# Transposes moved from TensorE and PSUM to DMA: a two-layer retention and sliding-window step on eight cores

## What is computed

```python
def retention_chunk(S, q, k, v, lg):          # chunks of 128 tokens, 4 heads, key 256, value 512
    scores = einsum('bihd,bjhd->bhij', q, k) * decay          # decay[i,j] = exp((i-j)*lg), i >= j
    o = einsum('bhij,bjhe->bihe', scores, v)
    o = o + einsum('bihd,bhde->bihe', q * exp((idx+1)*lg), S)
    k_dec = k * exp((C-1-idx)*lg)
    S_new = exp(C*lg) * S + einsum('bjhd,bjhe->bhde', k_dec, v)
# retention_mixer: y = (silu(g) * rms_norm(o)) @ w_out
# attention: q, k = rope(rms_norm(q, q_gain)), rope(rms_norm(k, k_gain)); 16 query and 4 key heads of 64
#   y = softmax([q k^T / 8, sink]) v @ w_out, window 128
# every block: x = x + mixer(rms_norm(x, gain)); x = x + swiglu(rms_norm(x, gain))
```

## Time and profile before

| | us |
|---|---|
| median of 3 runs (2007.52 to 2010.4) | 2008.47 |
| the profiled execution's own time | 2006.02 |
| its span, slowest core (core 7) | 2004.5 |
| spans of the 8 cores | 1994.1 to 2004.5 |
| PE busy, share of the span | 1886.5, 94% |
| DVE, ACT, POOL busy | 1083.5, 740.9, 258.7 |
| mean granted TensorE clock, core 7 | 0.979 |

### The profile page before, as it was taken

The page is one execution under the profiler, slowest core; times in us unless marked ns, Lnnn a source line. Parts: engine busy times, 40 slices in busy tenths (PEclk is TensorE's granted clock), DMA queues, the critical chain, the costliest instruction groups (busy, mean ns, idle before and its releaser), DMA issues.

```text
span 2004.5 us, 30003 instructions; the slowest of 8 cores (1994.1 to 2004.5 us)
## 1 busy us (share of the span) xinstructions
PE 1886.5 (94%) x10850; PEld 876.3 (44%) x10850; DVE 1083.5 (54%) x1544; ACT 740.9 (37%) x1201; POOL 258.7 (13%) x463
## 2 busy tenths in 40 slices
PE   4889999989989989999999998989989999999998
PEld 1434444434434434444444444444444444444444
DVE  3668677767758754334334467665653333343444
ACT  3555454455446761111111155665665111111111
POOL 2211101101111120000000014332331000000000
PEclk9889999999989999999999999999999999999999
DMA  9745743653552450533024113000064031240113
GB/s 183 186 106 133 159 122 112 161 130 125 137 137 103 121 143 15 96 50 64 12 37 60 20 33 64 1 1 4 1 90 64 1 64 22 42 64 0 33 43 132
DMA packets 103823, 153.80 MB, mean 77 GB/s; under 512 B 6464, under 2 KB 56640, under 8 KB 103616
## 3 DMA queue, kind: packets, MB, share of 16 engines
q0 software_dynamic: 59920, 59.91, 20.3%
q1 hardware_dynamic: 43760, 91.97, 13.9%
HBM read 167.08 MB, written 48.76 MB: 108 GB/s over the span
## 4 chain that ended last, share of the span: by engine, by line
PE 84%; DVE 4%; issue 4%; ACT 4%; DMA 2%; POOL 1%; SPq 0%; DVEq 0%; ACTq 0%; POOLq 0%
PE PS L705 81%; ACT R L719 4%; PE PS L711 3%; DVE R L726 3%; DVE R L736 1%; POOL R L726 1%; DMA R<-w_ret_out 1%; DMA R<-w_ffn_in 1%; DMA ss_out<-R 1%; DMA R<-xp 0%; DMA R<-state 0%; POOL R L730 0%; SPq L203 0%; POOL R L203 0%; DVE R L740 0%
## 5 line engine op out<-in xcount | busy, mean ns | idle before, releaser
L705 PE MATMUL PS<-R 128*128 128x512 bf16 (+7 forms) x9568 | 1826.8, 353 | 61.0 <-ACT R L719 32.5
L705 PEld LDWEIGHTS PS<-R 128*128 128x128 bf16 (+3 forms) x9568 | 796.9, 99 | 997.2 <-issue 204.6
L726 DVE TENSOR_TENSOR R<-R,PS 128x1024 f32<-128x1024 f32 (+3 forms) x530 | 484.5, 921 | 616.8 <-PE PS L705 586.1
L719 ACT ACTIVATE R<-PS 128x512 bf16<-128x512 f32 (+7 forms) x674 | 413.0, 626 | 1088.8 <-PE PS L705 999.2
L719 ACT ACTIVATE R<-R 128x1024 bf16<-128x1024 f32 (+3 forms) x302 | 289.3, 972 | 137.1 <-DVE R L726 57.7
L726 DVE TENSOR_TENSOR R<-PS,R 128x1024 bf16<-128x1024 bf16 (+7 forms) x270 | 179.2, 682 | 171.9 <-PE PS L705 105.2
L711 PE MATMUL PS<-R 128*128 128x128 bf16 (+1 forms) x1282 | 127.0, 225 | 50.6 <-ACT R L719 31.3
L736 DVE SCALAR_TENSOR_TENSOR R<-PS,R 128x512 f32<-128x512 f32 (+2 forms) x224 | 137.8, 638 | 59.7 <-POOL R L726 35.7
L726 POOL TENSOR_TENSOR R<-R 128x1 f32<-128x1 f32 (+5 forms) x238 | 150.3, 638 | 108.9 <-DVE R L726 86.4
L736 DVE SCALAR_TENSOR_TENSOR R<-R,PS 128x1024 f32<-128x1024 f32 x124 | 147.7, 1217 | 27.6 <-PE PS L705 17.3
L711 PEld LDWEIGHTS PS<-R 128*128 128x128 bf16 (+1 forms) x1282 | 87.8, 101 | 124.3 <-issue 98.3
(11 more groups left out here) (19 smaller groups left out, 42.2 us busy)
## 6 DMA issues: line engine op xcount, KB each, us to landing
R<-state SPq DMA_DIRECT2D x64, 512.0 KB, 4.3
ss_out<-R SPq DMA_DIRECT2D x64, 512.0 KB, 3.0
R<-w_ffn_in POOLq DMA_DIRECT2D x16, 1024.0 KB, 11.5
R<-xp SPq DMA_DIRECT2D x16, 512.0 KB, 13.8
R<-w_ret_in POOLq DMA_DIRECT2D x8, 1024.0 KB, 12.1
R<-w_ffn_out POOLq DMA_DIRECT2D x8, 1024.0 KB, 9.6
yp<-R SPq DMA_DIRECT2D x16, 512.0 KB, 3.8
R<-w_ffn_in POOLq DMA_DIRECT2D x8, 768.0 KB, 8.9
```

The costliest lines, as they stand in the source:

```text
L705: o = self.P.op("pe", lambda e: e.matmul(real(out), lhsT=lhsT, rhs=rhs, start=start, stop=stop), reads, writes, dur=max(0.029, self._fsz(o ...
L719: return self.P.op("act", lambda e: e.activation(out=real(out), in_=real(in_), func=func, **kw), reads, writes, dur=(0.38 if "accum_out" i ...
L726: return self.P.op(eng, lambda e: e.tensor_tensor(out=out, in0=real(in0), in1=real(in1), op=op), reads, writes, dur=self._vd(out, eng))
```

## The change

A new helper `dtr` issues a transposing DMA from SBUF to SBUF on SP's queue, with one of 8 semaphores ("xt") in turn. It replaces the PE transposes and the copy out of PSUM in five places: norms 1, 2 and 3 (DMA from hb into HT, then the gain product in place in HT, by DVE in norm 2 and by POOL in norms 1 and 3), gated heads, retention keys, attention's queries and keys, and attention's outputs. Norm 0, the sample keys of retention and the cached keys of attention keep PE. Since a DMA cannot scale, the decay of a key moves into the ACT copy of v; the mask decT, which v now meets too, becomes a constant per head on and above the diagonal. Keys are laid out chunk by chunk (kr), gated and oTg get two buffers each, the gate buffer sg4 two instead of four, and `gn_tr` is called right after `gn_elem` instead of a chunk later. The planner has a pipe of its own for these DMAs, at twice the rate.

```diff
-                s0 = max(st + 1.6, pipe[0])
-                pipe[0] = s0 + o.nbytes / DMA_RATE
-                fin = pipe[0] + 0.5
+                pi_ = 1 if o.slot[0] == "xt" else 0
+                s0 = max(st + 1.6, pipe[pi_])
+                pipe[pi_] = s0 + o.nbytes / DMA_RATE / (1 + pi_)
+                fin = pipe[pi_] + 0.5
...
-        decT[:, h, :] = np.where(diff >= 0, np.exp(-(i[:, None] + 1.0) * lg[h]), 0.0)
+        decT[:, h, :] = np.where(diff >= 0, np.exp(np.float32(-128.0) * lg[h]), 0.0)
...
+    def dtr(self, out, in_, reads, writes):
+        self.ndtr = (self.ndtr + 1) % 8
+        return self.P.dma("sp", out, in_, slot=("xt", self.ndtr), reads=reads, writes=writes, transpose=True)
...
+            if gi > 0:
+                ht = self.HT[:, :, t * 128:t * 128 + n]
+                self.dtr(ht, hb[0:n, :], [hk], [("HT", t)])
+                self.tt(ht, ht, self.gainT[:, gi, :].unsqueeze(2).broadcast_to([128, 8, n]), ALU.mult, [("HT", t), "gainT"], [("HT", t)],
+                        eng="dve" if gi == 2 else "pool")
+                return
...
-        kr = [A(f"kr{i}", [2, 512], BF16) for i in range(2)]
+        kr = [A(f"kr{i}", [4, 2, 128], BF16) for i in range(2)]
         ta = A("ta", [512], F32); tb = A("tb", [512], F32)
-        vc = [A(f"vc{i}", [512], BF16) for i in range(2)]; sg4 = A("sg4", [4, 512], BF16)
+        vc = [A(f"vc{i}", [512], BF16) for i in range(2)]; sg4 = A("sg4", [2, 512], BF16)
...
-        gated = A("gated", [512], BF16); oTg = A("oTg", [4, 128], BF16)
+        gateds = [A(f"gated{i}", [512], BF16) for i in range(2)]; oTgs = [A(f"oTg{i}", [4, 128], BF16) for i in range(2)]
...
+            gated, gk_ = gateds[i], f"gated{i}"
+            gq_.append(i)
             r_ = rst[:, i, :]; rk = ("rst", i)
-            self.act(gated[0:n, :], src, AF.Square, o_keys, ["gated", rk], scale=RDV ** -0.5, accum_out=r_[0:n, 0:1])
...
-                     o_keys + [rk, sgkey], ["gated"])
...
+                     o_keys + [rk, sgkey], [gk_])
...
         def gn_tr(n):
-            ti, tk = self.bank()
-            pb = self.psb(ti).rearrange("p (a b) -> p a b", a=8)
-            for ec in range(4):
-                self.tr(pb[:, ec, 0:n], gated[0:n, ec * 128:(ec + 1) * 128], ident[0:n, 0:n], ["gated", "ident"], tk)
-            self.act(oTg[:, :, 0:n], pb[:, 0:4, 0:n], AF.Copy, tk, ["oTg"])
+            i = gq_.pop(0)
+            oq_.append(i)
+            self.dtr(oTgs[i][:, :, 0:n], gateds[i][0:n, :], [f"gated{i}"], [f"oTg{i}"])
...
+            oi_ = oq_.pop(0)
+            oTg, otk = oTgs[oi_], f"oTg{oi_}"
...
-            rope(bi, bk, 512, tok0, kr[s % 2], f"kr{s % 2}", 1.0 / 16.0)
+            rope(bi, bk, 512, tok0, kr[s % 2].rearrange("p c a q -> p a c q"), f"kr{s % 2}", 1.0 / 16.0)
...
             bi, bk = proj_tm(f"rg{h}", 128, cidx * 128, [("HT", cidx)])
-            self.act(sg4[:, cidx % 4, :], self.psf(bi), AF.Silu, bk, [("sg4", cidx % 4)])
...
-                ti, tk = self.bank()
-                pb = self.psb(ti).rearrange("p (a b) -> p a b", a=8)
-                for hf in range(2):
-                    self.tr(pb[:, hf, :], kb[:, hf, c0:c0 + 128], ident, [kbk, "ident"], tk)
-                self.act(ktb, pb[:, 0:2, :].rearrange("p a b -> p (a b)"), AF.Copy, tk + ["kcol"], [ktk], scale=kcol[:, h:h + 1])
+                self.dtr(ktb.rearrange("p (a b) -> p a b", a=2), kb[:, cc, :, :].rearrange("p a b -> p (a b)"), [kbk], [ktk])
                 bi, bk = proj_tm(f"rv{h}", 128, cidx * 128, [("HT", cidx)])
-                self.act(vcb, self.psf(bi), AF.Copy, bk, [vck])
+                self.act(vcb, self.psf(bi), AF.Copy, bk + ["kcol"], [vck], scale=kcol[:, h:h + 1])
...
-                    self.mm(self.psf(si)[:, 0:128], kb[:, hf, c0:c0 + 128], qb[:, hf, c0:c0 + 128], hf == 0, hf == 1, [kbk, qbk], sk_)
+                    self.mm(self.psf(si)[:, 0:128], kb[:, cc, hf, :], qb[:, hf, c0:c0 + 128], hf == 0, hf == 1, [kbk, qbk], sk_)
...
-                if prev is not None:
-                    gn_tr(128)
...
                 gn_elem(128, oi, ok_, sgb, sgk, h)
+                gn_tr(128)
...
         def front_tr(n, fr, kT, kTk, qT, qTk):
             q_r, qrk, kd, kdk = fr
-            ti, tk = self.bank()
-            pb = self.psb(ti).rearrange("p (a b) -> p a b", a=8)
-            for m in range(2):
-                self.tr(pb[:, m, 0:n], kd[0:n, 2 * m:2 * m + 2, :].rearrange("p a b -> p (a b)"), ident[0:n, 0:n], [kdk, "ident"], tk)
-            self.act(kT, pb[:, 0:2, 0:n], AF.Copy, tk, [kTk])
-            ti, tk = self.bank()
-            pb = self.psb(ti).rearrange("p (a b) -> p a b", a=8)
-            for cc in range(8):
-                self.tr(pb[:, cc, 0:n], q_r[0:n, cc, :, :].rearrange("p a b -> p (a b)"), ident[0:n, 0:n], [(qrk, cc // 4), "ident"], tk)
-            self.act(qT, pb[:, :, 0:n], AF.Copy, tk, [qTk])
+            self.dtr(kT[:, :, 0:n], kd[0:n].rearrange("p a b -> p (a b)"), [kdk], [kTk])
+            self.dtr(qT[:, :, 0:n], q_r[0:n].rearrange("p a b c -> p (a b c)"), [(qrk, 0), (qrk, 1)], [qTk])
...
         def o_tr(n_):
             oT, oTk = oTs[0], "oT0"
             o_n, onk = o_ns[0], "o_n0"
-            ti, tk = self.bank()
-            pb = self.psb(ti).rearrange("p (a b) -> p a b", a=8)
-            for cc in range(8):
-                self.tr(pb[:, cc, :], o_n[:, cc, :, :].rearrange("p a b -> p (a b)"), ident, [(onk, cc // 4), "ident"], tk)
-            self.act(oT, pb, AF.Copy, tk, [oTk])
+            self.dtr(oT, o_n.rearrange("p a b c -> p (a b c)"), [(onk, 0), (onk, 1)], [oTk])
```

More of the change, by code:

```diff
@@ L287, in schedule @@
         last_form = [0]
-        pipe = [0.0]
+        pipe = [0.0, 0.0]
         total = len(allops)
@@ L634, in __init__ @@
         self.uid = 0
+        self.ndtr = 0
     def inp(self, name, shape):
@@ L958, in retention @@
         gcnt = [0]
+        gq_ = []
+        oq_ = []
         pend_nb = []
@@ L964, in rope @@
             a = ta[:, 0:n]; b_ = tb[:, 0:n]
+            o0, o1 = out[:, 0], out[:, 1]
+            av, bv = (a, b_) if len(out.shape) == 3 else (a.rearrange('p (c q) -> p c q', c=4), b_.rearrange('p (c q) -> p c q', c=4))
             self.stt(a, x1, scale, cs, ALU.mult, ALU.mult, [keys[0], ("rcos", tok0 // 512)], ["ta"])
             self.stt(b_, x2, scale, sn, ALU.mult, ALU.mult, [keys[1], ("rsin", tok0 // 512)], ["tb"])
-            self.tt(out[:, 0, 0:n], a, b_, ALU.subtract, ["ta", "tb"], [outkey])
+            self.tt(o0, av, bv, ALU.subtract, ["ta", "tb"], [outkey])
             self.stt(a, x2, scale, cs, ALU.mult, ALU.mult, [keys[1], ("rcos", tok0 // 512)], ["ta"])
             self.stt(b_, x1, scale, sn, ALU.mult, ALU.mult, [keys[0], ("rsin", tok0 // 512)], ["tb"])
-            self.tt(out[:, 1, 0:n], a, b_, ALU.add, ["ta", "tb"], [outkey])
+            self.tt(o1, av, bv, ALU.add, ["ta", "tb"], [outkey])
         def proj_fm(wname, n, tok0, htkeys):
@@ L992, in gn_elem @@
             gcnt[0] += 1
+            gated, gk_ = gateds[i], f"gated{i}"
+            gq_.append(i)
             r_ = rst[:, i, :]; rk = ("rst", i)
-            self.act(gated[0:n, :], src, AF.Square, o_keys, ["gated", rk], scale=RDV ** -0.5, accum_out=r_[0:n, 0:1])
+            self.act(gated[0:n, :], src, AF.Square, o_keys, [gk_, rk], scale=RDV ** -0.5, accum_out=r_[0:n, 0:1])
             self.rsq(r_[0:n, 2:3], r_[0:n, 0:1], n, [rk], epsc[0:n, ecol:ecol + 1], ["epsc"])
             self.stt(gated[0:n, :], src, r_[0:n, 2:3], sgbuf[0:n, :], ALU.mult, ALU.mult,
-                     o_keys + [rk, sgkey], ["gated"])
+                     o_keys + [rk, sgkey], [gk_])
         def gn_tr(n):
-            ti, tk = self.bank()
-            pb = self.psb(ti).rearrange("p (a b) -> p a b", a=8)
-            for ec in range(4):
-                self.tr(pb[:, ec, 0:n], gated[0:n, ec * 128:(ec + 1) * 128], ident[0:n, 0:n], ["gated", "ident"], tk)
-            self.act(oTg[:, :, 0:n], pb[:, 0:4, 0:n], AF.Copy, tk, ["oTg"])
+            i = gq_.pop(0)
+            oq_.append(i)
+            self.dtr(oTgs[i][:, :, 0:n], gateds[i][0:n, :], [f"gated{i}"], [f"oTg{i}"])
         def gn_out(h, n, xt):
             wo = self.W[f"ro{h}"]
+            oi_ = oq_.pop(0)
+            oTg, otk = oTgs[oi_], f"oTg{oi_}"
             if n == NS:
-                self.pair_out(xt, lambda i: wo[:, i, :], lambda i: ["oTg", self.wkey[f"ro{h}"]], lambda i: oTg[:, i, 0:n], 4)
+                self.pair_out(xt, lambda i: wo[:, i, :], lambda i: [otk, self.wkey[f"ro{h}"]], lambda i: oTg[:, i, 0:n], 4)
             else:
@@ L1194, in retention @@
         self.free("rcos", "rsin", "decT", "epsc", "kcol", "sdec", "rowmask", "qr0", "qr1", "kr0", "kr1", "ta", "tb",
-                  "vc0", "vc1", "sg4", "sTm0", "sTm1", "ktok0", "ktok1", "gated", "oTg", "Sf", "Sb", "rst", "qr_s", "kr_s",
+                  "vc0", "vc1", "sg4", "sTm0", "sTm1", "ktok0", "ktok1", "gated0", "gated1", "oTg0", "oTg1", "Sf", "Sb", "rst", "qr_s", "kr_s",
```

6 lines of the change are left out of this document (3 added, 3 removed).

## The result

The changed kernel takes **2075.59 us** (median of 4 runs, lowest 2073.72) against 2007.99 us for the kernel before on the same chip (4 runs): ratio **1.033**, 95% interval 1.031 to 1.035. The forecast was 1973 us. The profiled execution has a span of 2074.9 us on core 3, against 2004.5 before: +70.4. In the cores' list the mean granted clock of TensorE is 0.952 to 0.957, before 0.977 to 0.982. Some runs of a kernel are far slower, with a lower mean clock on one half of the chip or on both; ratios leave those out, and a time called "compared" is the median of the runs that its ratio uses.

What follows compares the result with a forecast made beforehand. The prediction took PE to bind almost everywhere; -57 - 10 + 5 + 6 + 20 = -36 us against 2006.0 gave 1970, and with 2.5 for the median of the runs 1973 us, range 1937 to 2110.

Steps and rivals of the forecast that it cites:

- PE's share, -57 us: On PE's path: 1106 of 1282 transposing instructions go, at 52 ns each, 57 us gained.
- The gain on ACT's waits (-10): PE's waits before transposes and attention matmuls, partly for copies of transposed tiles: 10 us gained, ends 0 and 24.
- Landing 3.5 and 3.0 us: Transposing DMAs on SP's queue: assumed landing of a 128x1024 tile and of a gated head's 128x512 tile.
- the packet rival (8.1 us): Transposes pay by the packet: 128x1024 lands in 8.1 us, 128x512 in 4.9; kernel 2112 us; chance 0.26.
- how much does PE tolerate: Room for a transpose's landing, from PE's order: 3.1 us at attention outputs, 2.3 and 3.4 us at gated heads.
- These 26 us of stall: PE's forecast stalls for transposes: 20 us at gated heads, 6 us at attention outputs, 0 at norms and keys.
- POOL's gain product, 5 us: 34 products of 128x1024 on POOL, some 2.5 us each, costing 5 us in all; ends 0 and 30.
- SP's issue, 0.38 us each: SP's time to issue each of 233 transposes, taken from plain DMAs; nobody waits for it at that price.
- SP blocks in retention: Rival: transposes behind state loads in SP's order cost 56 us instead of 6, about 2023 us; chance 0.14.
- either end that I drew from the Trainium skill: Two pages on 128x1024 transposes: 10.5 us and about 2160 us in all, or 1.0 us and about 1945.
- my own list: Expected signs: 176 L711 left, landings 2.5 to 4 us, small DMA waits, faster attention, unchanged feed-forward.
- The signs that were to show the forecast wrong: Median landing above 4.2 us, SP's queue busy most of an attention block, or retention waits over 60 us.

Runs made afterwards that it cites:

- e8: Changed kernel with only the gated heads' transposes back on TensorE: 2044.6 us compared, ratio 1.015 to the kernel before.
- e3: Changed kernel, same order, weight pieces from the ninth on loading only their first row block: 2019.44 us, ratio 1.006.
- e4: Kernel before the change, own order, weight pieces from the ninth on loading only their first row block: 1999.7 us compared, ratio 0.997.
- e5: Changed kernel, planner counting transposing DMAs in the one pipe of all DMAs, without the halved time per byte: 2015.03 us, ratio 1.000.
- e6: Changed kernel with the gain products of norms 1 to 3 left out: 2052.62 us, ratio 1.018.
- e13: Changed kernel with its separate planner pipe kept, only SP's planned time per transpose set to 1.2 us: 2085.95 us, ratio 1.030.
- e9: Changed kernel with one shared planner pipe and SP's planned time per transpose set to 1.2 us: 2007.01 us, ratio 0.990.
- e15: The kernel of e9 again with more rounds: 1998.17 us (6 runs), ratio 0.989 to the kernel before.

## Why the prediction was wrong

- **PE's share, -57 us:** right. 176 instructions are left, and the busy time gives 47. The gain on ACT's waits (-10) came in part and was lost elsewhere: ACT's row before ordinary matmuls falls from 16.8 us to 11.7 in attention, but grows from 32.5 to 41.6 over the span.
- **Landing 3.5 and 3.0 us:** right as a median (3.1 over all), and so the packet rival (8.1 us) fell, though it had the sign. The pieces are 256-byte packets as it feared, 1024 for a 128x1024 tile. But if the whole growth of q1's share is theirs, it gives (0.245 × 2074.9 - 0.139 × 2004.5) × 16 / 145,824 = 0.025 us for one, a quarter of the 0.102 it took from the long packets.
- **The step that failed** is "how much does PE tolerate": "Stall of gated heads: 19 × (3.0 + 0.35 - 2.3) = 20 us, the second group 0", and 6 for attention outputs, 0 for norms and keys "unless the queue itself is full". These 26 us of stall were the term that failed. PE stood 58.9 to 69.3 us for transposes directly, gated heads came to 31 + 14 = 45 us by e8, and PE's idle time grew by 106.6 in all. Two things are in it. I set one usual landing against each distance, and where weight pieces were in flight the landings shown took 11 to 16 us; with the weights thinned 47 of the 67 us were gone (e3, e4). And even then PE stood 38.5 to 46.1 us for transposes, so the distances of this order didn't cover shorter landings either; how these waits split over gated heads, keys, norms and outputs isn't shown. The trace of the kernel before had two warnings. A state load's median of 4.3 us hid a longest of 9.6 to 13.1 over the cores (80 to 800 us), and these pieces were on POOL's queue, which I didn't take as the company of a transpose:

```profile
R<-w_ffn_in POOLq DMA_DIRECT2D x16, 1024.0 KB, 11.5
R<-w_ret_in POOLq DMA_DIRECT2D x8, 1024.0 KB, 12.1
```

- **The order wasn't questioned.** The distances were read from the changed kernel's order, but that order was made by a planner that in the same diff had been told that transposes never queue behind other transfers. Put right, the same instructions take 60 us less (e5). It was in the diff and had no term or rival.
- **POOL's gain product, 5 us:** its duration was right (2.0 against 2.5), the wait in front was not: 23 us (e6), within my ends of 0 and 30, and 6 once the order is mended.
- **SP's issue, 0.38 us each:** measured 1.2, and up to 9.0 under weight pieces. Mending it in the plan alone takes back none of the 67 us (e13), but 8 to 17 once the pipe is right (e9, e15); what the issue time itself costs on the chip wasn't isolated. The rival "SP blocks in retention" had the right engine and the wrong wait: SP's wait for stored states fell from 163.4 us to 31.6.
- **The clock** had no term. More idle time goes with a lower mean grant (0.952 to 0.957 against 0.977 to 0.982); the same matmuls took 10.5 us more beside it. In e15 the same matmuls take 1816.7 us at a mean of 0.965 (its core 6), less than before at 0.979, so mean clock and matmul time don't go together one to one, and no more is claimed.
- **The pages.** The trace doesn't bear out either end that I drew from the Trainium skill. "VectorE: DVE Perf Modes", section "The three transpose paths", gives 1309 ns for 128x128; eight squares landed in 3.1 us, not in proportion. "DMA: Bandwidth & Descriptors", section "Latency and other measured facts", gives 261 GB/s for transposes with a non-contiguous middle dimension; 64 packets of 0.025 us on each of 16 engines are an estimate of 1.6 us for 256 KB, or 160 GB/s, beside this kernel's other transfers.

By my own list, 1106 fewer, the landing and the full feed-forward parts came true; PE's waits for DMA in attention (16.6 us against "under 15") and in retention (51.3 against "under 30") did not, and attention took 9.5 us more instead of less. The signs that were to show the forecast wrong, a median landing above 4.2 us or over 60 us of waits in retention, didn't come either: a median can't show a tail, and less than 60 us was enough to lose.

**Open:** why the issue of a transpose holds SP for up to 9 us while weight pieces fly. The long landing isn't peculiar to transposes. Over the eight cores the longest landing of a state load in retention was 9.6 to 13.1 us in the kernel before, 10.1 to 11.6 in the changed one, and 6.0 to 7.9 in it with thin weights (each from 80 us on), all at medians near 4. But the issue of a state load took 1.9 us at most in the changed kernel. Fewer small packets per transpose or weight pieces in smaller parts weren't tried.

## What to carry to other kernels

Price a transfer that stands on the path by its landing in the company that it keeps, not by the median: look up which large loads are in flight where its reader waits, and the longest landing of a plain load there. When a change moves work to another engine and also edits the planner's costs, test the two apart first; here the moved work was worth some 10 us of gain under a sound plan, and the planner's edit cost 60. And a consumer placed on an in-order engine behind a DMA (the gain product on POOL) costs its wait, not its duration.
